# Opening a streaming encoder step by three token tiles, with the first B tile and the time-step tile projected in turn and the time-step chain laid token by token on 128 partitions

## The reference, cut to what matters

```
h    = rmsnorm(x) * g_pre                       # 1056 tokens x 1024
proj = h @ w_in                                 # u, v, za, zb, xbc (12 tiles of 128), dt_raw (16 columns)
xbc  = silu(causal_dwconv(xbc, 4 taps))         # 8 tiles of x, 2 of B, 2 of C
dt   = softplus(dt_raw + dt_bias)               # per token, 16 heads
acs  = cumsum over each block of 128 tokens of dt * (-exp(a_log))
```

## Time and profile before

| what | value |
|---|---|
| median of 3 runs | 1663.06 us (1661.76 to 1663.37) |
| the profiled execution's own time | 1661.99 us |
| its span in the trace | 1660.2 us |
| TensorE busy | 1576.7 us, 95% of the span |
| VectorE, ScalarE, GpSimd busy | 813.7, 668.9, 440.5 us |
| mean granted clock of TensorE | 0.984 |

### The profile page before, as it was taken

How to read it: one execution, slowest core, us unless ns; L and a number is a source line. 1 busy time by engine, 2 the same in 40 slices (tenths; PEclk the granted TensorE clock), 3 DMA queues, 4 the chain that set the end, 5 groups by cost and what they waited for, 6 DMA issues and landing times.

```text
span 1660.2 us, 26649 instructions
## 1 busy us (share of the span) xinstructions
PE 1576.7 (95%) x9562; PEld 1454.8 (88%) x9562; DVE 813.7 (49%) x1753; ACT 668.9 (40%) x1243; POOL 440.5 (27%) x267
## 2 busy tenths in 40 slices
PE   5899999998999999999999899999999999998898
PEld 5899999998999999978888788989898889887676
DVE  5755677664885323135565633434433443435432
ACT  6432333232223332334455344444444544445321
POOL 1113444333221121144443221312122221215000
PEclk9999999998999999999999899999999999999999
DMA  4121122212102111053555436523241323213121
GB/s 146 40 66 57 56 70 71 84 43 55 51 25 54 39 39 50 25 178 127 184 175 152 65 64 57 49 51 74 41 70 38 65 41 67 49 50 133 52 89 70
DMA packets 128740, 121.06 MB, mean 73 GB/s; under 512 B 9706, under 2 KB 112500, under 8 KB 128684
## 3 DMA queue, kind: packets, MB, share of 16 engines
q1 hardware_dynamic: 128684, 120.30, 29.6%
HBM read 101.61 MB, written 18.66 MB: 72 GB/s over the span
## 4 chain that ended last, share of the span: by engine, by line
PE 80%; DVE 7%; issue 5%; ACT 5%; DMA 1%; POOL 1%; SPq 0%; ACTq 0%; DVEq 0%; POOLq 0%
PE PB L719 75%; PE PB L723 6%; DVE NRML L1744 2%; ACT L1240 1%; ACT L1630 1%; DMA XS<-in_x_prompt_dram 1%; ACT WH L1234 1%; ACT NRMH L1234 1%; ACT SB L1707 0%; DMA nf_rows<-NFROW 0%; DVE DTROW L1744 0%; ACT PT L1234 0%; DVE XT L1751 0%; DVE KALL L1751 0%; DVE SB L1748 0%
## 5 line engine op out<-in xcount | busy, mean ns | idle before, releaser
L719 PE MATMUL PB<-HH,WH 128*128 128x352 f32 x1872 | 621.5, 332 | 14.9 <-ACT XR L1254 6.0
L719 PE MATMUL PB<-HH,WL 128*128 128x352 f32 x1872 | 605.0, 323 | 0.0
L719 PE MATMUL PB<-HL,WH 128*128 128x352 f32 x1872 | 604.5, 323 | 0.0
L719 PEld LDWEIGHTS PB<-HH,WH 128*128 128x128 f32 x1872 | 355.3, 190 | 28.9 <-issue 20.2
L719 PEld LDWEIGHTS PB<-HL,WH 128*128 128x128 f32 x1872 | 356.1, 190 | 0.0
L719 PEld LDWEIGHTS PB<-HH,WL 128*128 128x128 f32 x1872 | 354.7, 189 | 0.0
L604 POOL TENSOR_TENSOR WL<-WRAW,WH 128x1024 fp32r<-128x1024 f32 x82 | 200.7, 2449 | 564.5 <-ACT WH L1234 556.9
L1234 ACT ACTIVATE WH<-WRAW 128x1024 fp32r<-128x1024 f32 x112 | 117.8, 1052 | 27.5 <-DMA WRAW<-in_w_in_even_dram 19.5
L1707 ACT ACTIVATE SB<-SB,small 128x128 f32<-128x128 f32 (+8 forms) x72 | 53.8, 748 | 80.5 <-DVE small L1748 80.5
L1744 DVE TENSOR_TENSOR Y<-PB,Y 128x128 f32 (+2 forms) x72 | 20.2, 280 | 133.2 <-PE PB L719 133.1
L719 PE MATMUL PB<-PT,VTOK 128*128 128x128 f32 (+2 forms) x624 | 81.9, 275 | 0.1
(11 more groups left out here) (290 smaller groups left out, 2424.1 us busy)
## 6 DMA issues: line engine op xcount, KB each, us to landing
WRAW<-in_w_out_even_dram SPq DMA_DIRECT2D x48, 512.0 KB, 3.5
WRAW<-in_w_in_even_dram SPq DMA_DIRECT2D x44, 512.0 KB, 3.8
WRAW<-in_w_in_odd_dram SPq DMA_DIRECT2D x32, 512.0 KB, 8.1
ACSB<-acs_rows SPq DMA_DIRECT2D x16, 528.0 KB, 4.9
NFB<-nf_rows SPq DMA_DIRECT2D x8, 656.0 KB, 3.7
XS<-in_x_prompt_dram SPq DMA_DIRECT2D x8, 512.0 KB, 5.7
XT<-in_x_prompt_dram SPq DMA_DIRECT2D x8, 512.0 KB, 4.7
x_rows<-OG SPq DMA_DIRECT2D x8, 512.0 KB, 5.3
```

Source lines behind the costliest of these rows:

```text
L719: return pe.matmul(out, lhsT, rhs, start=start, stop=stop)
```

## The change

It does two things. Removed lines of the opening and of the time-step chain are those printed above; they are mostly left out below, and so are fences.

1. **Opening by three.** Transposes go by three token tiles (`TRIPLES`: 384, 384 and 288 columns) through a ring of three banks. Norms of later tiles are interleaved with the copies of earlier ones on ScalarE and VectorE. The first B tile becomes weight tile 0, the time-step tile number 1. TensorE projects chunk c of both in turn, with the transposes of the next three token tiles between the steps. The raw time steps go to `DTRAW`, B's chunks to `XR`.
2. **Token by token.** The raw time steps are transposed once (9 blocks), and the chain runs on 128 partitions by 9 x 16 columns. The running sum within a block is a matmul with a triangle of ones (`TRI`), the block's end one with all ones. The sums are turned back (2 transposes) for the store, in nine transfers. `conv(0)` comes before the chain, and its SiLU before chunk reads of the second B tile. ScalarE reads each next tile ahead of the SiLU of the one before.

```diff
-W_DT, W_BC, W_XZ, W_V, W_UZ, W_OE, W_F, W_QKVZ, W_OO = 0, 1, 5, 21, 29, 45, 93, 94, 126
+W_DT, W_XZ, W_V, W_UZ, W_OE, W_F, W_QKVZ, W_OO = 1, 5, 21, 29, 45, 93, 94, 126
+W_BC = (0, 2, 3, 4)
...
+TRIPLES = [(0, 3 * P), (3 * P, 3 * P), (6 * P, 2 * P + DEC)]
+RING = (3, 4, 5)
...
+                load_w(tile_no(W_BC[0], 1, 0), even(XBC0 + 8 * P))
+            if b == 5:
                 load_w(tile_no(W_DT, 1, 0), even(DT0, HEADS_B), HEADS_B)
...
-        sp.dma_start(DTB[0:HEADS_B, :], dt_bias[0].unsqueeze(1)).then_inc(S("par_in"), 16)
-        sp.dma_start(AL[0:HEADS_B, :], a_log[0].unsqueeze(1)).then_inc(S("par_in"), 16)
+        sp.dma_start(DTBB[:, :], dt_bias[0:1, :].broadcast_to([P, HEADS_B])).then_inc(S("par_in"), 16)
+        sp.dma_start(ALB[:, :], a_log[0:1, :].broadcast_to([P, HEADS_B])).then_inc(S("par_in"), 16)
...
-        sp.wait_ge(S("dtc"), 3)
-        sp.dma_start(acs_rows, ACSROW[:, :]).then_inc(S("acs_stored"), 16)
-        sp.wait_ge(S("acs_stored"), 16)
-        sp.wait_ge(S("dt_turn"), 1)
+        sp.wait_ge(S("dt_rows"), 2)
+        for b in range(NB):
+            sp.dma_start(acs_rows[:, b * P:(b + 1) * P], ACSR[b * HEADS_B:(b + 1) * HEADS_B, :]) \
+                .then_inc(S("acs_stored"), 16)
+        sp.dma_start(acs_rows[:, SEQ:TOK], ACSS[:, :]).then_inc(S("acs_stored"), 16)
+        sp.wait_ge(S("acs_stored"), 16 * 9)
...
-        for q, (b0, nb, rows) in enumerate(QUADS):
...
+        def x_turn(g, k):
+            i = g * KT + k
+            if k == 0:
+                pe.wait_ge(S("xn"), 3 * g + 3)
+            if i >= len(RING):
+                pe.wait_ge(S("h_lo"), i - len(RING) + 1)
+            for j in range(3):
+                b = 3 * g + j
+                rows = sample_rows(b)
+                last = turn(PB[RING[i % 3]][:, j * P:j * P + rows], XS[0:rows, b, k * P:(k + 1) * P])
+            last.then_inc(S("x_t"), 1)
+        def first_step(w, c, bank, k):
+            if k == 0:
+                pe.wait_ge(S("w_low"), w + 1)
+            pe.wait_ge(S("h_lo"), c * KT + k + 1)
+            cols = slice(c * CH, (c + 1) * CH)
+            mm(PB[bank][:, 0:CH], WH[:, w, k, :], HH[:, k, cols], start=k == 0, stop=False)
+            mm(PB[bank][:, 0:CH], WH[:, w, k, :], HL[:, k, cols], start=False, stop=False)
+            last = mm(PB[bank][:, 0:CH], WL[:, w, k, :], HH[:, k, cols], start=False, stop=k == KT - 1)
+            if k == KT - 1:
+                last.then_inc(S("p_chunk"), 1)
+        for k in range(KT):
+            x_turn(0, k)
+        for k in range(KT):
+            if k >= 4:
+                x_turn(1, k - 4)
+            first_step(W_BC[0], 0, 0, k)
+        for k in range(KT):
+            if k < 4:
+                x_turn(1, k + 4)
+            first_step(W_DT, 0, 7, k)
+        for k in range(KT):
+            if k >= 4:
+                x_turn(2, k - 4)
+            first_step(W_BC[0], 1, 1, k)
+        for k in range(KT):
+            if k < 4:
+                x_turn(2, k + 4)
+            first_step(W_DT, 1, 6, k)
+        for k in range(KT):
+            first_step(W_BC[0], 2, 2, k)
+        for k in range(KT):
+            first_step(W_DT, 2, 5, k)
+        w1 = tile_no(W_BC[1], 1, 0)
+        project_chunk(w1, w1, 0, HH, HL)
+        pe.wait_ge(S("c_read2"), W_DT + 1)
+        pe.wait_ge(S("dtc"), 1)
+        for b in range(NB + 1):
+            last = turn(PB[3][:, b * HEADS_B:(b + 1) * HEADS_B], DTRAW[:, b * P:(b + 1) * P])
+        last.then_inc(S("dt_turn"), 1)
+        project_chunk(w1, w1, 1, HH, HL)
+        project_chunk(w1, w1, 2, HH, HL)
+        pe.wait_ge(S("dtc"), 4)
+        steps = DTA[:, :, :].rearrange("p b h -> p (b h)")
+        mm(PB[4][:, 0:9 * HEADS_B], TRI[:, :], steps)
+        mm(PB[4][:, 256:256 + 9 * HEADS_B], ONES[:, :], steps).then_inc(S("dt_turn"), 1)
+        w2 = tile_no(W_BC[2], 1, 0)
+        project_chunk(w2, w2, 0, HH, HL)
+        pe.wait_ge(S("dtc_a"), 4)
+        turn(PB[3][:, 0:P], TOKQ[:, 3, 0:NB, :].rearrange("p b h -> p (b h)"))
+        turn(PB[3][0:HEADS_B, P:P + DEC], TOKQ[0:DEC, 3, NB, :]).then_inc(S("dt_turn"), 1)
+        project_chunk(w2, w2, 1, HH, HL)
+        project_chunk(w2, w2, 2, HH, HL)
+        project(tile_no(W_BC[3], 1, 0), tile_no(W_BC[3], 1, 0), HH, HL)
...
+        x_square(0)
+        x_square(1)
+        x_root(0)
+        x_square(2)
+        x_root(1)
+        x_root(2)
+        act.wait_ge(S("rows_turn"), 1)
...
+        copy(DCOL[:, :], PB[3][:, P:P + 8]).then_inc(S("cols"), 1)
...
+        split_high(tile_no(W_BC[0], 1, 0))
+        x_square(3)
+        x_high(0, range(0, 4))
+        x_square(4)
+        x_root(3)
+        x_high(0, range(4, 8))
+        x_square(5)
+        x_root(4)
+        x_root(5)
...
+        split_high(tile_no(W_DT, 1, 0))
+        x_square(6)
+        x_high(1, range(0, 4))
+        x_square(7)
+        x_root(6)
+        x_high(1, range(4, 8))
+        x_square(NB)
+        x_root(7)
+        x_root(NB)
+        x_high(2, range(0, 8))
...
+        raw = whole(DTRAW, HEADS_B)
+        for c in range(3):
+            read_first(c, parted(XR, 3, SAMP), c, 2 * c + 1)
+            if c == 2:
+                act.wait_ge(S("w_raw0"), loads_of_slot(tile_no(W_BC[1], 1, 0)))
+                copy(WH[:, 0, :, :], WRAW[:, 0, :, :]).then_inc(S("w_high"), 1)
+            read_first((7, 6, 5)[c], raw, c, 2 * c + 2, HEADS_B)
+        split_high(tile_no(W_BC[2], 1, 0))
+        conv_silu(0, BT[:, 0, :])
         load_ln_exp()
...
+        act.activation(EAL[:, :], ALB[:, :], ACT.Exp).then_inc(S("dtc_a"), 1)
+        read_chunk(tile_no(W_BC[1], 1, 0), parted(XR, 3, SAMP), 0)
+        act.wait_ge(S("dtc"), 2)
+        act.activation(DTE[:, :, :], DTN[:, :, :], ACT.Exp).then_inc(S("dtc_a"), 1)
+        act.wait_ge(S("dtc"), 3)
+        order(act.activation(DTL[:, :, :], DTW[:, :, :], ACT.Ln))
...
+        act.activation(DTN[:, :, :], DTL[:, :, :], ACT.Exp, scale=-1.0).then_inc(S("dtc_a"), 1)
+        read_chunk(tile_no(W_BC[1], 1, 0), parted(XR, 3, SAMP), 1)
+        read_chunk(tile_no(W_BC[1], 1, 0), parted(XR, 3, SAMP), 2)
+        split_high(tile_no(W_BC[3], 1, 0))
+        act.wait_ge(S("dt_turn"), 2)
+        sums = PB[4][:, 0:9 * HEADS_B].rearrange("p (b h) -> p b h", h=HEADS_B)
+        ends = PB[4][:, 256:256 + 9 * HEADS_B].rearrange("p (b h) -> p b h", h=HEADS_B)
+        order(act.activation(DECB[:, :, :].rearrange("p h b -> p b h"), ends, ACT.Exp))
+        copy(TOKQ[:, 3, :, :], sums).then_inc(S("dtc_a"), 1)
...
+        act.wait_ge(S("dtc_a"), 4)
+        order(act.activation(TOKQ[:, 2, :, :], TOKQ[:, 3, :, :], ACT.Exp))
...
+        act.wait_ge(S("dtc"), 5)
+        act.activation(DTE[:, :, :], DTD[:, :, :], ACT.Exp).then_inc(S("dtc_a"), 1)
+        act.wait_ge(S("dt_turn"), 3)
+        copy(ACSR[:, :], PB[3][:, 0:P]).then_inc(S("dt_rows"), 1)
+        copy(ACSS[:, :], PB[3][0:HEADS_B, P:P + DEC]).then_inc(S("dt_rows"), 1)
+        act.wait_ge(S("conv"), 2)
+        read_chunks(tile_no(W_BC[2], 1, 0), parted(XR, 3, SAMP))
+        split_high(tile_no(W_XZ, 1, 0))
+        conv_silu(1, BT[:, 1, :])
+        act.wait_ge(S("conv"), 3)
+        read_chunks(tile_no(W_BC[3], 1, 0), parted(XR, 3, SAMP))
+        split_high(tile_no(W_XZ + 1, 1, 0))
+        conv_silu(2, CT[:, 0, :])
+        conv_silu(3, CT[:, 1, :])
         act.wait_ge(S("conv"), 4)
...
+        x_mean(0)
+        x_mean(1)
+        x_norm(0)
+        x_mean(2)
+        x_norm(1)
+        x_norm(2)
+        dve.wait_ge(S("rows_in"), 112)
+        dve.tensor_copy(DEXP[:, :, :], DSM[:, :].unsqueeze(2).broadcast_to([8, 2, HP])).then_inc(S("dexp"), 1)
+        x_mean(3)
+        x_low(0, range(0, 4))
+        x_mean(4)
+        x_norm(3)
+        x_low(0, range(4, 8))
+        x_mean(5)
+        x_norm(4)
+        x_norm(5)
+        x_mean(6)
+        x_low(1, range(0, 4))
+        x_mean(7)
+        x_norm(6)
+        x_low(1, range(4, 8))
+        x_mean(NB)
+        x_norm(7)
+        x_norm(NB)
+        x_low(2, range(0, 8))
...
+        dve.memset(DTRAW[:, TOK:], 0.0).then_inc(S("dtc"), 1)
...
+        order(ts(TRI[:, :], MASKT[:, :], 0.0, None, ALU.is_ge))
+        conv(0, 8, tile_no(W_BC[0], 1, 0))
+        dve.wait_ge(S("dtc_a"), 1)
...
+        order(ts(EALB[:, 0:NB, :], EAL[:, :].unsqueeze(1).broadcast_to([P, NB, HEADS_B]), -1.0, None, ALU.mult))
...
+        dve.wait_ge(S("dt_turn"), 1)
+        turned = PB[3][:, 0:9 * HEADS_B].rearrange("p (b h) -> p b h", h=HEADS_B)
+        order(tt(DTX[:, :, :], turned, DTBB[:, :].unsqueeze(1).broadcast_to([P, 9, HEADS_B]), ALU.add))
...
+        order(ts(DTN[:, :, :], DTX[:, :, :], -1.0, None, ALU.mult))
...
+        tt(DTN[:, :, :], DTX[:, :, :], DTN[:, :, :], ALU.min).then_inc(S("dtc"), 1)
+        dve.wait_ge(S("dtc_a"), 2)
+        ts(DTW[:, :, :], DTE[:, :, :], 1.0, None, ALU.add).then_inc(S("dtc"), 1)
+        dve.wait_ge(S("dtc"), 3)
+        order(ts(DTC[:, :, :], DTW[:, :, :], -1.0, None, ALU.add))
...
```

(44 more changed lines are left out.)

101 lines of the change are left out of this document (37 added, 64 removed).

## The result

The changed kernel takes 1649.35 us (median of 4 runs, 1649.07 to 1651.91), the kernel before 1663.21 beside it. The ratio is 0.992, with a 95% interval of 0.9904 to 0.9936: faster by 13.9 us of medians, more than the 0.2% that can be told from no change. The forecast was 1649.0 within 1646.5 to 1656.5.

The account below looks back on a forecast made before the run. TensorE, busy 1480 of 1539 us after 121.6 us, bounds the kernel; the change moves how early it gets there. Terms sum to -14.0: 1661.99 to 1648.0, plus 1.07 for the median, 1649 us; range 1646.5 to 1656.5.

Parts of the forecast that it names:

- Term A: Opening: both first tiles done at 52.2 us instead of 57.1, so -4.9 us, bounds -3 and -6.
- the gate at 24: Opening: TensorE waits for the norms of the second three token tiles, expected ready at 24.7 us.
- the step of the third group: Opening, third group of token tiles: a step of three transposes and three matmuls was expected to take 0.81 us.
- Term B: Second B tile's weights, split after the last B chunk is read, covered by only one chunk: +0.5 us (0 to +0.9).
- Term C: TensorE's wait for ScalarE's read into XR: 6.0 us and 1.5 of slow restart removed, -7.5 us.
- term D: Small transposes before a projection: 1.4 us instead of 4.2, slow clock stretch gone too, -2.8 us; bound -1.2.
- E: TensorE's wait for the time-step chain's sums, ready at 65.5 us against 64.8: +0.7 us (0 to +3).
- The two splits on `conv(0)`: First convolution: two GpSimd weight splits (50.1 and 53.8) fall on it, ending it between 56.4 and 59.1 us.
- Term F: Later convolutions have 1 to 2 us to spare: 0 us (0 to +3, if two more splits fall on them).
- gate the opening: Rival: norms hold up the opening, so its gain is 0 to 1 us instead of 5; 1653 to 1654 us, chance 0.17.
- The convolution chain: Rival: convolutions become the bound, leaving 7.3 us of the gain, 1656 us; chance 0.15.
- the cold mixed steps: Rival: opening's steps of matmuls and transposes run at 1.2 GHz throughout, costing 25 us, so 1674 us; chance 0.03.

Follow-up runs that it names:

- the two halves: Each part of the change alone, against the kernel before: new opening with old chain 1668.07 us, ratio 1.0031; old opening with new chain 1655.98 us, ratio 0.9953.
- the third: Third profile of the unaltered changed kernel, from its last repeat run beside the kernel before; that run's median was 1649.76 us.

## Why the prediction was right, point by point

**The sum.** It forecast -14.0 us; the start of the CB stage moved by -13.2 in the traces, the median by -13.9. That the median hits the forecast to 0.4 us is luck. Taken as the sum was made, from profiled execution to profiled execution, 1648.0 was forecast and 1649.58 came, -12.4: 0.8 us because the terms before the CB stage were too good, 0.7 because the untouched part was longer in this trace. The 1.07 us that the forecast added for the median was not there after the change, where the median lies 0.23 below the profiled execution. The mechanism came out as said: no TensorE wait above 0.4 us from 25 to 101 us, the CB stage at 101.7 and the z projection at 108.6, where 101 and 108 were named.

**Term A, the opening (-4.9): measured -3.7.** Both tiles are done at 43.16 + 6.42 + 3.84 = 53.4 us, not 52.2. The start, the ring of three and the gate at 24 were right within 0.7 us, on the early side, and by the end of the time-step tile's first chunk TensorE was 0.9 early (33.3 against 34.2). What was mis-sized is the step of the third group, taken as 0.81 and in truth 1.08: eight of them are 2.1 us late, which leaves 1.2. The run with 128 rows shows that the 32-row transposes cause it.

**Term B, the second B tile's weights (+0.5): 0.2.** The chain of read, split and split took 4.0 us, where the forecast went from 48.4 to 52.7, so 4.3; TensorE's chunk beside it took 3.84 both times.

**Term C, the stall (-7.5): right.** No wait and no slow clock is left. That it hangs on the chain, not on the opening, the two halves show.

**Terms D and E, small transposes and sums (-2.8 and +0.7): together -2.2, forecast -2.1.** From 53.62 to 101.69 there are 48.07 us, 12 chunks are 46.08, so 1.99 is left for 9 + 2 transposes, two matmuls and the wait, where 4.2 stood before. E alone was 0.2: TensorE reached the block sums 1.3 us later than worked out and the chain 0.6, so they met. The two splits on `conv(0)` were predicted and came. Of the rest of term D, the nine and the two transposes took 0.66 and 0.23 us, and no slow stretch followed.

**Term F, the later convolutions (0): right.** ScalarE never kept TensorE waiting there. The split that the forecast had over `conv(1)` did lengthen it (the copy above), and its reads came when TensorE was ready.

**The rivals.** The norms do gate the opening, at 24.08, but earlier than feared. The convolution chain did not become the bound; two added operations show how near the time-step chain ahead of it was. TensorE worked at half rate up to 23.4 us in this profile (25 in the third) and no longer, so the cold mixed steps did not come. That the parts might not be independent was not among the rivals. It did not matter for the sum, but one part alone would have been forecast wrongly from these terms: -4.9 for the opening, where it costs 5.3.

## What to carry to other kernels

Interleaving two producers delays the completion of the first. It pays only if what hangs on that first one is short enough, so cost each part of a change alone as well as together. Where a time-step row of 16 partitions by 1056 goes through thirteen operations, turning it to 128 partitions by 144 makes a two-input one a quarter (1.25 us to 0.31), and the turning must be few blocks: nine left the clock alone here, 36 in a row did not. Here a chain whose end just met its reader gained next to nothing by being 2 us shorter and lost at once when longer.

## What the runs showed of the hardware

- Three transposes of which one has 32 rows, between matmuls over 128 rows, cost 0.27 us more per step than three of 128 rows. Doing useless rows was cheaper.
- 36 transposes of 16 x 128 blocks in 2.4 us, without any gap around them, were followed by some 3 us at 1.2 GHz (granted clock 0.50).
- One GpSimd split (2.4 us) that met the convolution's three multiplies lengthened them by 2.0 us, two by 4.0. A copy of three columns under a split took 1.80 us instead of 0.17 and ended with it. The split loses too when it comes second: the one at 54.89, started inside a running multiply, took 3.40 us instead of 2.4.
- The view's clock column can read 1.00 at the start of a trace while matmuls run at half rate: 0.29 us between starts against 0.16.
